# Attention and hybrid mixer: values and output projections from high and low parts, mixers' splits three panels ahead, input products summed in one bank half

## What is computed

```python
h = h + 0.5 * rmsnorm(swiglu(rmsnorm(h, gn[0]), ffn1_w_in[i], ffn1_w_out[i]), gn[1])
hn = rmsnorm(h, gn[2])
m = mixer(hn)                      # HGRN, differential attention, pooling, HGRN | hybrid, recurrent
h = h + rmsnorm(m, gn[3])
h = h + 0.5 * rmsnorm(swiglu(rmsnorm(h, gn[4]), ffn2_w_in[i], ffn2_w_out[i]), gn[5])
```

```python
q, k, v = jnp.split(x @ w_in, 3, axis=-1)
...
w = p[:, :, 0] - lam_full * p[:, :, 1]
o = rmsnorm(einsum('bhqk,bhkv->bhqv', w, v), subln_w) * (1.0 - lam_init)
return o.reshape(B, S, D_MODEL) @ w_out
```

```python
return jnp.concatenate([y_ssm, o], axis=-1) @ w_out
```

## Time and profile before

| | |
|---|---|
| median of 3 runs | 3132.32 us (3131.69 to 3132.42) |
| the profiled execution | 3131.68 us, span 3130.0 us |
| TensorE busy | 3088.1 us, 99% |
| VectorE busy | 2185.8 us, 70% |
| ScalarE busy | 1681.7 us, 54% |
| read from HBM | 531.0 MB, 170 GB/s over the span |
| mean granted clock of TensorE | 0.998 |

### The profile page before, as it was taken

One profiled execution on the slowest core, in us unless ns is written; L12 is line 12 of the kernel. 1 busy time (PEld: TensorE's weight loads), 2 busy tenths in 40 slices (PEclk: granted clock), 3 DMA queues, 4 the chain that ended last, 5 costly groups with the idle time before them and its releaser, 6 DMA issues.

```text
span 3130.0 us, 44746 instructions
## 1 busy us (share of the span) xinstructions
PE 3088.1 (99%) x18100; PEld 2702.6 (86%) x18100; DVE 2185.8 (70%) x2635; ACT 1681.7 (54%) x2069; POOL 4.0 (0%) x22
## 2 busy tenths in 40 slices
PE   9999999999999999999999999999999999999998
PEld 8888888888888888888888888888888888888887
DVE  7768675867586775685866867586774675867774
ACT  6566654645464554454656665464642454646553
POOL 0000000000000000000000000000000000000000
PEclk9999999999999999999999999999999999999999
DMA  6543454554345454455454345455432454554453
GB/s 234 188 168 142 148 189 175 188 188 162 122 175 188 175 189 168 160 190 189 175 190 167 135 151 189 172 194 189 161 143 98 158 189 175 189 189 161 162 189 121
DMA packets 75356, 534.78 MB, mean 171 GB/s; under 512 B 8480, under 2 KB 8608, under 8 KB 10784
## 3 DMA queue, kind: packets, MB, share of 16 engines
q1 hardware_dynamic: 75168, 532.07, 46.7%
HBM read 530.99 MB, written 1.05 MB: 170 GB/s over the span
## 4 chain that ended last, share of the span: by engine, by line
PE 92%; DVE 4%; ACT 2%; DVEq 1%; issue 1%; DMA 0%; POOL 0%; POOLq 0%; ACTq 0%; SPq 0%
PE pp L2030 18%; PE pp L2029 18%; PE pp L2031 9%; PE pp L2028 9%; PE pp L2192 5%; PE pp L2053 4%; PE pm L2030 4%; PE pm L2029 4%; PE pp L2055 2%; PE pm L2031 2%; PE pm L2028 2%; PE pp L2023 2%; PE pp L2021 2%; PE pp L2022 2%; PE pp L2083 1%; PE pp L2235 1%
## 5 line engine op out<-in xcount | busy, mean ns | idle before, releaser
L1772 DVE TENSOR_TENSOR wlo<-raw,whi 128x2048 fp32r<-128x2048 f32 x461 | 1054.4, 2289 | 409.4 <-ACT whi L1572 408.8
L1572 ACT ACTIVATE whi<-raw 128x2048 fp32r<-128x2048 f32 x461 | 879.7, 1911 | 273.8 <-DMA raw<-weights 273.1
L2030 PE MATMUL pp<-xs,whi 128*128 128x512 f32 x2296 | 917.3, 400 | 3.7 <-DVE tsum L1852 3.3
L2029 PE MATMUL pp<-xs,whi 128*128 128x512 f32 x2296 | 909.5, 396 | 0.0
L2028 PE MATMUL pp<-xs,wlo 128*128 128x256 f32 x2296 | 640.3, 279 | 0.0
L2031 PE MATMUL pp<-xs,wlo 128*128 128x256 f32 x2296 | 637.6, 278 | 0.0
L1662 ACT ACTIVATE corr<-pp 128x512 f32<-128x512 f32 x335 | 199.3, 595 | 620.5 <-PE pp L2029 594.2
L2028 PEld LDWEIGHTS pp<-xs,wlo 128*128 128x128 f32 x2296 | 431.5, 188 | 104.4
L2031 PEld LDWEIGHTS pp<-xs,wlo 128*128 128x128 f32 x2296 | 433.4, 189 | 96.1
L2030 PEld LDWEIGHTS pp<-xs,whi 128*128 128x128 f32 x2296 | 436.4, 190 | 15.0 <-DVE tsum L1852 12.4
L2029 PEld LDWEIGHTS pp<-xs,whi 128*128 128x128 f32 x2296 | 431.4, 188 | 0.0
(11 more groups left out here) (362 smaller groups left out, 4127.8 us busy)
## 6 DMA issues: line engine op xcount, KB each, us to landing
raw<-weights SPq DMA_DIRECT2D x503, 1024.0 KB, 4.8
raw<-weights SPq DMA_DIRECT2D x8, 256.0 KB, 6.9
h<-x_by_feature SPq DMA_DIRECT2D x4, 256.0 KB, 6.0
out<-h SPq DMA_DIRECT2D x4, 256.0 KB, 2.5
vec<-vectors SPq DMA_DIRECT2D x1, 264.0 KB, 2.7
lamrow<-diff_lambda SPq DMA_DIRECT2D x1, 128.0 KB, 12.2
skiprow<-ssm_d SPq DMA_DIRECT2D x1, 8.0 KB, 12.3
```

The lines of the kernel that those rows point to most:

```text
L1572: nc.scalar.activation(whi[:, slot, :], raw[:, slot, :], ACT.Copy).then_inc(sem("weights_hi"), 1)
L1772: v.tensor_tensor(wlo[:, slot, :], raw[:, slot, :], whi[:, slot, :].bitcast(F32), ALU.subtract).then_inc(sem("weights_lo"), 1)
L2029: return mm(bank, whi[:, slot, c:c + P], x_k, start=False, stop=stop)
L2030: mm(bank, whi[:, slot, c:c + P], x_k, start=start, stop=False)
```

## The change

1. In differential attention and the hybrid the value panels and the output projections are made from parts. Their panels, 20 in all, are split as the others are; `token_product` and `whole_input` have no user left. The output projection's input gets parts too: a step `hi` on ACT writes `yhi`, a step `lo` on DVE (in the hybrid, `take` itself) writes `mixlo`; the state-space half gets its parts in `xs`.
2. In all mixers the input panels after the first two are made by `summed_product`; there is no correction to copy and add, and DVE scales straight from the bank.
3. In all mixers panel p is followed by the split of p + 3 in place of p + 4, and in the second panel no split is left. ACT waits for a panel's product only where it reads it.
4. In the hybrid's `long_out` the state-space half goes through the first two panels' tiles together.

```diff
-            subs.append(dict(kind=DIFF, gain=g + 2, layer=l, segs=[Segment("diff_in", 3 * D // PC, tokens=(4, 9, 10, 11)), out_proj("diff_out")]))
+            subs.append(dict(kind=DIFF, gain=g + 2, layer=l, segs=[Segment("diff_in", 3 * D // PC, tokens=(4, 9, 10, 11), parts=True), out_proj("diff_out", True)]))
...
-                Segment("hyb_qkv", 3 * D // PC, first_half=1, tokens=(0, 1, 10, 11)),
-                Segment("hyb_out", 2 * D // PC, reads=0, whole=True)]))
+                Segment("hyb_qkv", 3 * D // PC, first_half=1, tokens=(0, 1, 10, 11), parts=True),
+                Segment("hyb_out", 2 * D // PC, reads=0, whole=True, parts=True)]))
...
-                 9: ["wT4", "rstd0", "exp5"], 10: ["wT5", "exp6", "exp7"], 11: ["wT6", "square1", "wT7"]},
+                 9: ["wT4", "rstd0", "exp5"], 10: ["hi0", "wT5", "exp6", "exp7"], 11: ["wT6", "square1", "wT7"]},
...
-                 8: ["weights4", "max5"], 9: ["weights5", "max6", "norm0"], 10: ["weights6", "out1", "max7", "weights7"],
+                 8: ["weights4", "max5"], 9: ["weights5", "max6", "norm0"], 10: ["weights6", "lo0", "out1", "max7", "weights7"],
...
+                elif name == "hi":
+                    act.wait_ge(sem("at_normed"), n + 1)
+                    nc.scalar.activation(yhi[:, 2 * n:2 * n + 2, :], mix[:, 0, 2 * n:2 * n + 2, :], ACT.Copy).then_inc(sem("at_hi"), 1)
...
+                elif name == "lo":
+                    q = slice(2 * n, 2 * n + 2)
+                    dve.wait_ge(sem("at_hi"), n + 1)
+                    v.tensor_tensor(mixlo[:, 0, q, :], mix[:, 0, q, :], yhi[:, q, :].bitcast(F32), ALU.subtract
+                                    ).then_inc(sem("at_lo"), 1)
...
+                elif name == "hi":
+                    act.wait_ge(sem("fox_out"), n + 1)
+                    act.wait_ge(sem("seg_out_read"), min(n + 6, KD))
+                    nc.scalar.activation(yhi[:, n, :], pm[:, 3, 0:T], ACT.Copy).then_inc(sem("fox_hi"), 1)
...
-            for name in "wT4 exps6 wT5 exps7 wT6 square1 wT7".split():
+            for name in "wT4 hi3 exps6 wT5 hi4 exps7 wT6 hi5 square1 wT7 hi6 hi7".split():
...
+            for k in range(KD):
+                act.wait_ge(sem("hyb_normed"), k + 1)
+                nc.scalar.activation(xs[:, k, 0:T], mix[:, 6, k, :], ACT.Copy).then_inc(sem("hyb_hi"), 1)
             read_out(s["segs"][2], s)
...
-                    dve.wait_ge(sem("fox_out"), n + 1)
-                    v.tensor_copy(mix[:, 3, n, :], pm[:, 3, 0:T]).then_inc(sem("fox_out_read"), 1)
+                    dve.wait_ge(sem("fox_hi"), n + 1)
+                    v.tensor_tensor(mixlo[:, 3, n, :], pm[:, 3, 0:T], yhi[:, n, :].bitcast(F32), ALU.subtract
+                                    ).then_inc(sem("fox_out_read"), 1)
...
+            normed(0)
+            for k in range(1, KD):
+                normed(k)
+                low(k - 1)
+            low(KD - 1)
             read_out(s["segs"][2], s)
...
                     long = seg.panels > 4
+                    if seg.parts:
+                        split(seg.g0 + 3)
+                        if long:
+                            split(seg.g0 + 4)
                     for p in range(3):
                         act.wait_ge(sem("panel_done"), seg.g0 + ((3, 4, 6)[p] if long else p + 1))
                         square_output(s, p)
                         scale_output(s, p)
-                        if not long or p:
+                        if seg.parts and long and p < 2:
+                            split(seg.g0 + 5 + p)
+                            if p:
+                                split(seg.g0 + 7)
+                        elif seg.parts and long:
+                            split(seg.g0 + seg.panels)
+                            split(seg.g0 + seg.panels + 1)
+                        elif not long or p:
                             split(seg.g0 + seg.panels + p - long)
...
-                    if after_first is not None and p < 2:
-                        split(seg.g0 + p + AHEAD - 1)
-                    if after_first is None or p >= 2:
-                        split(seg.g0 + p + AHEAD)
+                    split(seg.g0 + p + (AHEAD if closing else AHEAD - 1))
...
                     if p in seg.tokens:
                         hook(p)
-                        split(seg.g0 + p + AHEAD)
+                        split(seg.g0 + p + AHEAD - 1)
                         continue
...
+                    if opening and p < 2:
+                        v.tensor_tensor(dst(p), t2[half], r2, ALU.mult).then_inc(sem("opened"), 1)
+                    else:
+                        dve.wait_ge(sem("panel_done"), seg.g0 + p + 1)
+                        v.tensor_tensor(dst(p), in_banks[half][:, :, 0:T], r2, ALU.mult).then_inc(sem("panel_out"), 1)
+                    if opening and p == 0:
+                        split(seg.g0 + AHEAD)
+                    elif not opening or p >= 2:
+                        split(seg.g0 + p + AHEAD - 1)
...
+            def out_tile(bank, g, c, x, k, start, stop):
+
+                if len(x) == 1:
+                    return mm(bank, raw[:, g % SLOTS, c:c + P], x[0][:, k, :], start=start, stop=stop)
+                x_hi, x_lo = x[0][:, k, :], x[1][:, k, :]
+                mm(bank, whi[:, g % SLOTS, c:c + P], x_hi, start=start, stop=False)
+                mm(bank, whi[:, g % SLOTS, c:c + P], x_lo, start=False, stop=False)
+                return mm(bank, wlo[:, g % SLOTS, c:c + P], x_hi, start=False, stop=stop)
...
                 for pair in range(2):
-                    pe.wait_ge(sem(f"raw_landed_{(seg.g0 + 2 + pair) % SLOTS}"), landings(seg.g0 + 2 + pair))
...
+                    out_weights(seg, seg.g0 + 2 + pair)
+                for k in range(KD - 2):
+                    tail_ready(k)
+                    for pair in range(2):
+                        for ft in range(2):
+                            half(pair, 1, ft, k)
```

More of the change, by code:

```diff
@@ L69, in ffn, with out_proj @@
             Segment(f"ffn_in_{n}", 2 * FF // PC), Segment(f"ffn_out_{n}", 11, wide=7)])
-    def out_proj(name):
-        return Segment(name, D // PC, reads=0, whole=True)
+    def out_proj(name, parts=False):
+        return Segment(name, D // PC, reads=0, whole=True, parts=parts)
     subs = []
@@ L100, in build @@
         subs.append(ffn(9 + 2 * l, g + 4))
-    panels = reads = fills = ffns = 0
+    panels = reads = copies = fills = ffns = mixers = 0
     splits_before, whole_panels = [], set()
@@ L108, in build @@
         s["ls0"], s["it"], s["xw"] = log1ps, hgrns, token_mixers
+        s["opening"] = mixers
+        mixers += s["kind"] != FFN
         s["tokens"] = any(seg.tokens for seg in s["segs"])
@@ L117, in build @@
         for seg in s["segs"]:
-            seg.g0, seg.r0, seg.t0 = panels, reads, token_panels
+            seg.g0, seg.r0, seg.c0, seg.t0 = panels, reads, copies, token_panels
+            copies += seg.reads if s["kind"] == FFN else 2 * (seg is s["segs"][0])
             token_panels += len(seg.tokens)
@@ L121, in build @@
                 splits_before.append(g - len(whole_panels) - min(g, 2))
-                if seg.whole or g - seg.g0 in seg.tokens and not seg.parts:
+                if (seg.whole or g - seg.g0 in seg.tokens) and not seg.parts:
                     whole_panels.add(g)
@@ L192, in banks_of, with projected @@
             return out_banks[p - seg.wide] if seg.wide else in_banks[(p + seg.first_half) % 2]
+        def projected(engine, s, seg, p):
+            if seg is s["segs"][0] and p < 2:
+                engine.wait_ge(sem("opened"), 2 * s["opening"] + p + 1)
+            else:
+                engine.wait_ge(sem("panel_out"), seg.read(p) + 1)
         def two(buf):
@@ L709, in pe_diff @@
             step = pe_at_step(pe, s)
-            products(s["segs"][0], xs, first=lambda: first_of(s), sums=lambda: column_sums(s), hook=at_hook("pe", step),
-                     whole_inputs=s["xw"] + 1)
+            products(s["segs"][0], xs, first=lambda: first_of(s), sums=lambda: column_sums(s), hook=at_hook("pe", step))
+            parts = yhi, mixlo[:, 0]
             def normed(k):
-                pe.wait_ge(sem("at_normed"), k // 2 + 1)
+                pe.wait_ge(sem("at_lo"), k // 2 + 1)
             everywhere = ((0, 0), (0, 1), (1, 0), (1, 1))
@@ L718, in pe_diff @@
             begin(s, 1)
-            rows(s, mix[:, 0], (0,), everywhere, range(KD), normed)
+            rows(s, parts, (0,), everywhere, range(KD), normed)
             step("sums", 1)
@@ L1741, in read_out @@
                             hook(1)
-                            split(seg.g0 + AHEAD + 1)
                     elif hook is not None:
@@ L1910, in read_out @@
                 if seg.whole:
+                    if seg.parts:
+                        for p in range(3, seg.panels):
+                            split(seg.g0 + p)
                     for p in range(3):
@@ L1923, in read_out @@
                         hook(p)
```

(24 more changed lines are left out.)

137 lines of the change are left out of this document (70 added, 67 removed).

## The result

The changed kernel takes 3144.35 us (median of six; 3140.46 to 3147.21) against 3132.01 of the kernel before, a ratio of 1.0039 with a 95% interval from 1.003 to 1.0049: slower by 12.3 us. The forecast was 3134 with a range up to 3142. It missed, on the slow side. The profiled execution took 3144.24 us (span 3142.5), 12.56 us more than the one of before.

The account below looks back on a forecast made before the run. PE, busy 99% of the span, was taken to bound the kernel. Savings of 29.5 us against waits of 10.3 (attention) and 16.3 (hybrid) and 4.8 for the clock gave +1.9 us: 3134 us, range 3117 to 3142.

Parts of the forecast that it names:

- the walked waits: New PE waits found by following ACT's and DVE's queues: 10.3 us in attention, 16.3 us in the hybrid.
- turn 7: Attention, before the first output rows: PE waits 5.8 us for ACT's transposed weights, delayed by splits.
- the tail: Hybrid, before the tail panels: PE waits 7.3 us for normalisations, a table load and the fourth panel's split.
- the sixth panel: Hybrid output: PE waits 4.1 us because ACT splits this panel only after the third panel's product is handled.
- The 0.5 us two heads on: Hybrid, last panel of values: a further 0.5 us wait two heads after the 3.5 us one.
- upper bound of 20: Hybrid's new waits: 16.3 us forecast, with bounds of 11 and 20.
- within 3 us: Sign to look for: attention and hybrid each take within 3 us of their time before.
- 752 x (354 - 348): Summed input products in all mixers: three matmuls cost 4.1 us more than the old form, bounds 0 to 12.
- third rival: Summed form on inputs runs at the values' 364 ns: +7.5 us, 3142, chance 0.06.
- I take 1.2 each: Half clock behind the four long waits in attention and hybrid: 4.8 us in all, bounds 0 to 6.8.
- second rival: Each of the four long waits brings two half-clock stretches, costing 3.4 us each: +8.8 us, 3143, chance 0.17.
- first rival: ACT and DVE find slack, so half the waits and clock loss are absent: 3118, chance 0.22.

Follow-up runs that it names:

- e9: The kernel before with only the value panels made by high and low parts: 3131.27 us, ratio 0.9996.
- e2: The changed kernel with the mixers' input products back in the old form, one matmul of 512 columns and one of 256: 3137.08 us, ratio 1.0017.
- e1: The changed kernel with the hybrid's fourth output panel split ahead of the normalisations: 3133.66 us, ratio 1.0006.
- e6: The changed kernel with four of the hybrid's output panel splits moved and its sum of squares ahead of the next sublayer's splits: 3119.75 us, ratio 0.9960.
- e10: The changed kernel with attention's splits placed as steps where their engine would wait anyway: 3136.80 us, ratio 1.0011.
- e4: The changed kernel with the hybrid's sum of squares on DVE ahead of the splits for the next sublayer: 3138.06 us, ratio 1.0021.
- e8: The changed kernel with 192 unused bytes ahead of the input's buffer, which moves the hidden buffer too: 3130.58 us, ratio 0.9998.
- e13: The changed kernel with input and hidden buffers both 320 bytes past a multiple of 512: 3126.61 us, ratio 0.9984.
- e11: The kernel before with input and hidden buffers both 320 bytes past a multiple of 512: 3123.03 us, ratio 0.9969.
- e14: Not labelled in the text; apparently the changed kernel with the input's buffer at 0, 192 or 256 past a multiple of 512 (3137.1, 3117.6 or 3138.4 us).

## Why the prediction failed, step by step

**Right: PE's savings.** Values: 9.0 us (e9) for 8.7. Output projections, by difference: 17.6 of work in all, less the values' 9.0 and plus the 7.3 of the summed form (e2), leaves 15.9 for 15.0.

**Right: the walked waits.** All but one came at their places, ended by the instruction named, nearly to their length: turn 7 5.65 us (5.8 forecast), the second panel behind it 0.67 (0.6), attention's last rows 0.98 (0.8), its third output panel 0.86 (0.8), the fifth head's turn 1.03 (0.9), its output 3.54 (3.5), the tail 7.50 (7.3), the sixth panel 4.31 (4.1). The 0.5 us two heads on did not come, and attention's panels 5 to 10 waited 1.7 us where 2.3 was estimated. For the fifth head DVE's timeline after shows the walk's own words, the split ahead of the take:

```profile
2393.88 2.28 DVE L1827 TENSOR_TENSOR wlo<-raw,whi 128x2048 fp32r<-128x2048 f32 x1
2396.25 0.42 DVE L1377 TENSOR_TENSOR mixlo<-pm,yhi 128x256 fp32r<-128x256 f32 x1
```

That the splits' order is the cause is shown by moving them, which took the waits away (e1, e6, e10); at the fifth head's output 1.3 us of 3.5 stayed in e6.

**Wrong, and the largest: the walk of the tail stopped one wait too early.** "Next, the sixth panel" was its last step; the prediction noted that "the first split of this stage, at 2436.44, served the next sublayer", and did not ask what that split becomes when three output panels stand before it. It moved from 2436 to 2455 us, beside the end of PE's last panel, and DVE's sum of squares is queued behind the low parts of two such splits. That is 4.1 us of waits (3.3, 0.4, 0.5) and 2.0 of slow matmuls; e4 measures 6.3. With it the hybrid's waits are 20.5 us, over the upper bound of 20, and the hybrid is 10.8 us longer than before, where "within 3 us" was the sign (attention is 3.0 longer).

**Wrong: "752 x (354 - 348)".** The form costs 7.3 us (e2) where 4.1 was taken; its row came from another buffer, and e8 and e13 show that the buffer's address carries the difference. The bound of 12 us held it. Against the third rival stood "the same operands in the same order"; that left out where they lie. Its 364 ns was nearer to the 360 measured than the forecast's 354, but it was a row of the values' form: a near hit without the cause.

**Wrong in size: the clock.** "I take 1.2 each" for four waits; they cost 1.7, 1.6, 2.2 and 1.5 us of slow matmuls, 7.0 for 4.8. The second rival, two stretches per wait, named nearly the time measured (3143), which is luck: its length of half clock came true in part (three of the five waits had 6.8 us of it, two had 3.4), its price did not. PE was idle in part of the longer stretches (busy 3.97, 4.75 and 5.71 of 6.82 us in the windows above), and one of 6.8 cost 1.7 to 2.2 and not 3.4; the rest of its 8.8 us is made up by the missed wait and the summed form. Nor does it "decide from waits longer than the one traced": 3.3 us brought 6.8 of half clock, 4.3 brought 3.4.

**Wrong, small:** of the 4.9 us of HGRN's and the short waits 4.1 went, and attention's waits are 0.8 below the walk.

Together: 6.1 (the missed wait with its clock) + 3.2 (summed form) + 2.2 (clock of the four) + 0.8 (short waits) - 0.8 (attention) - 1.2 (PE's other savings) + 0.2 (the opening's slow matmuls) = 10.5 of the 10.4 us between 1.9 and 12.3. The first rival, that the cover holds, falls with the waits at their places.

## What to carry to other kernels

Work that goes from the bounding engine to engines with idle time is free only if it is queued where they would have waited: the same change was 12 us slower in one order of its splits and sums and 12 us faster in another (e6). When a walk of queued work finds new waits, follow each moved instruction to the end of the stage and into the next; here the work pushed back last was the wait that was missed. And before a pitch is carried from one matmul to another, compare where their operands lie.

## What the runs showed of the hardware that was not expected

- Address of the operand that is streamed past the loaded weights (here the inputs). A product of three fp32r matmuls of 256 columns took 340 to 360 ns, and one of 512 and 256 took 345.1 to 348.5, with nothing changed but the buffer's place by multiples of 64 bytes. At 320 bytes the first takes 340 or 353 ns, panel by panel. Moving it was worth 8.4 us to the kernel before (e11) and 17.7 us to the changed one (e13), more than the change itself did.
- The same wait does not always bring the half clock. Before the hybrid's third panel PE stood 3.3 us in three kernels: the clock fell for 3.4 us in the earlier trace rows, for 6.8 us in e9, and not at all in e11, where the windows around and behind that wait are at full clock:

```profile
2231.00:2234.80 3.80, 0.60 (x4) 0.29 (x2) 2.82 (x2) 3.80 (x5) 0.00 (x0) 1.00 0.46 151
2235.50:2239.00 3.50, 3.50 (x23) 3.07 (x22) 3.35 (x5) 1.99 (x2) 0.00 (x0) 1.00 0.13 54
```

  Nor did the waits at the fifth head's output (PE idle for 3.3 us) and at the sum of squares (3.1) bring it in e14, where they begin at 2390.0 and 2454.9 us:

```profile
2392.00:2402.00 10.00, 8.20 (x68) 8.00 (x69) 5.53 (x13) 3.95 (x11) 0.00 (x0) 1.00 0.01 2
2454.00:2464.00 10.00, 6.92 (x56) 6.66 (x55) 6.79 (x7) 2.62 (x4) 0.00 (x0) 1.00 0.10 26
```

  A wait of this length is best priced with a range, from nothing to 2.9 us (the most one stretch of slow matmuls cost, in e10), and kernels a few us apart are to be compared by their work and waits as well as by their time.
